# Idle products ahead of four norms and of the last down product, a tenth expert slot, and finer waits ahead of three expert loads

## What is computed

```python
for l in range(2):
    h = rmsnorm(x, g[0]);  y = mixer_l(h);           x = x + rmsnorm(y, g[1])
    h = rmsnorm(x, g[2]);  y = relu(h @ w1)**2 @ w2;  x = x + rmsnorm(y, g[3])
mod = silu(c) @ w_ada + b_ada                    # sh1, sc1, ga1, sh2, sc2, ga2
h  = modulate(rms_norm(x, g_norm1), sh1, sc1)
z  = h @ w_in;   merged = gate_a * (attn @ w_pa) + gate_b * (conv @ w_pb)
x  = x + ga1 * (merged @ w_o)
h2 = modulate(rms_norm(x, g_norm2), sh2, sc2)
x  = x + ga2 * moe(h2)      # 32 experts; silu(xb @ w1[e]) * (xb @ w3[e]) @ w2[e]
```

## Time and profile before

| | |
|---|---|
| median of 3 executions | 1529.51 us (1523.59, 1529.51, 1529.6) |
| the profiled execution, its own time | 1525.64 us |
| its span, first to last instruction | 1523.8 us |
| mean granted TensorE clock | 0.92 |
| TensorE busy, share of the span | 1283.0 us, 84% |
| VectorE busy | 557.2 us, 37% |
| ScalarE busy | 213.4 us, 14% |
| GpSimd busy | 83.5 us, 5% |
| DMA, mean over the span | 247 GB/s, 376.79 MB |
| expert loads (`<-in_w`) | 92 of 2048 KB and 8 of 1024 KB |

### The profile page before, as it was taken

One profiled execution on the slowest core, in us unless ns is written; L12 is line 12 of the kernel. 1 busy time (PEld: TensorE's weight loads), 2 busy tenths in 40 slices (PEclk: granted clock), 3 DMA queues, 4 the chain that ended last, 5 costly groups with the idle time before them and its releaser, 6 DMA issues.

```text
span 1523.8 us, 13457 instructions
## 1 busy us (share of the span) xinstructions
PE 1283.0 (84%) x5716; PEld 789.1 (52%) x5716; DVE 557.2 (37%) x732; ACT 213.4 (14%) x357; POOL 83.5 (5%) x77
## 2 busy tenths in 40 slices
PE   7999998999999988999999989998746646636646
PEld 4856747885446754888444778556312212212212
DVE  5478422546344732256436484415101001001001
ACT  3321211110011411111001123112100000000000
POOL 0047100000010001000001100000000000000000
PEclk9999998999999998999998999997878868778788
DMA  8633335884443333587543433476699999999996
GB/s 319 183 120 111 111 124 207 282 309 170 177 166 111 111 124 125 194 303 247 187 173 111 166 111 111 166 299 253 287 428 427 428 428 428 428 428 427 428 428 260
DMA packets 93611, 376.79 MB, mean 247 GB/s; under 512 B 6992, under 2 KB 7664, under 8 KB 81648
## 3 DMA queue, kind: packets, MB, share of 16 engines
q1 hardware_dynamic: 92832, 373.80, 63.5%
q0 software_dynamic: 576, 2.10, 0.4%
q10 hardware_dynamic: 144, 0.04, 0.0%
HBM read 374.88 MB, written 1.05 MB: 247 GB/s over the span
## 4 chain that ended last, share of the span: by engine, by line
PE 70%; DMA 19%; DVE 5%; SPq 2%; ACT 2%; issue 2%; POOL 1%; POOLq 0%; DVEq 0%; ACTq 0%
PE PS L853 15%; PE PS L863 13%; PE PS L665 11%; DMA weights<-in_w 10%; DMA proj_rows<-in_w 9%; PE PS L707 8%; PE PS L648 8%; PE PS L1074 5%; PE PS L1105 2%; PE PS L618 2%; SPq L483 1%; PE PS L1038 1%; PE PS L823 1%; PE PS L1046 1%; PE PS L764 1%
## 5 line engine op out<-in xcount | busy, mean ns | idle before, releaser
L853 PE MATMUL PS<-normalised,weights 128*128 128x256 f32 x1024 | 225.9, 384 | 1.6 <-DVE normalised L1495 1.6
L1074 PE MATMUL PS<-weights,arena 128*32 128x512 f32 x464 | 141.3, 710 | 90.0 <-DMA arena<-in_w 56.8
L853 PEld LDWEIGHTS PS<-normalised,weights 128*128 128x128 f32 x1024 | 197.5, 193 | 30.0 <-DVE normalised L1495 2.4
L863 PE MATMUL PS<-weights,arena 128*128 128x512 f32 x384 | 167.4, 592 | 0.0
L665 PE MATMUL PS<-weights,normalised 128*128 128x256 f32 x696 | 155.1, 380 | 3.2 <-DVE weights L1540 2.5
L665 PEld LDWEIGHTS PS<-weights,normalised 128*128 128x128 f32 x696 | 131.2, 190 | 24.9 <-issue 6.4
L648 PE MATMUL PS<-weights,normalised 128*128 128x512 f32 x288 | 131.0, 614 | 2.7 <-DVE normalised L1495 2.0
L707 PE MATMUL PS<-weights,arena 128*128 128x512 f32 x288 | 125.1, 594 | 4.9 <-issue 4.1
L1074 PE MATMUL PS<-arena 128*32 128x512 f32 x256 | 90.0, 733 | 45.7 <-DMA proj_rows<-in_w 22.8
L863 PEld LDWEIGHTS PS<-weights,arena 128*128 128x128 f32 x384 | 73.0, 190 | 91.0 <-issue 90.9
L2057 DVE TENSOR_TENSOR arena<-arena,PS 128x512 f32<-128x512 f32 x8 | 8.4, 1047 | 291.2 <-PE PS L1074 291.2
(11 more groups left out here) (314 smaller groups left out, 1447.3 us busy)
## 6 DMA issues: line engine op xcount, KB each, us to landing
weights<-in_w SPq DMA_DIRECT2D x40, 2048.0 KB, 26.1
weights<-in_mlp_w SPq DMA_DIRECT2D x32, 2048.0 KB, 7.8
arena<-in_w SPq DMA_DIRECT2D x22, 2048.0 KB, 25.0
proj_rows<-in_w SPq DMA_DIRECT2D x20, 2048.0 KB, 25.4
proj_rows<-in_w_ada SPq DMA_DIRECT2D x12, 2048.0 KB, 8.2
weights<-in_ev_w_in SPq DMA_DIRECT2D x10, 2048.0 KB, 8.4
weights<-in_w_in SPq DMA_DIRECT2D x10, 2048.0 KB, 7.9
normalised<-in_w SPq DMA_DIRECT2D x10, 2048.0 KB, 24.7
```

The lines of the kernel that those rows point to most:

```text
L853: last = mm(PS[:, 4 + 2 * h + j // 2, (j % 2) * T:(j % 2 + 1) * T], wn(s)[:, k, j * P:(j + 1) * P], HT[:, k, :], start=(k == 0), stop=(k = ...
L863: last = mm(PS[:, bank, :], lhs[:, k0 + i, rows], rhs[:, i, :], start=(g == 0 and i == 0), stop=(g == NGRP - 1 and i == 1))
L1074: last = mm(PS[CAP * x:CAP * (x + 1), 4 + kind, :], XG[:, k, CAP * x:CAP * (x + 1)], w[:, k, :], start=(k == 0), stop=(k == KT - 1), tile_ ...
```

## The change

- `keep_warm(bank, n)` issues n products of the identity with 512 columns of the constants into a bank of PSUM that nobody reads before it is written anew. It is called with n = 6 at the head of `mlp` (norms 1 and 3, bank 7), with 2 ahead of norm 2 and with 3 ahead of norm 4 (bank 6, after a wait on `y_rows`), and with 1 in the last group (bank 4).
- In the last group the scatter of the first half moves from behind the loop to a place ahead of the second half's down product, with the waits on `ex_swT` and `ex_y0`; behind the loop only the second half's is left.
- `MOE_SLOTS` has ten entries. The new slot 9 is 4096 columns of the array `arena` from column 2048 on. What lay there in the expert phase moves into the arrays of the residual rows, the head gains and the first gated rows.
- Expert blocks 4, 5 and 6 wait for the last `part_sum`, `merged` 2 and `mg_T` 3; blocks 7 and 8 for the two W_O blocks, block 9 for `h2_raw` 4. Before, 4 and 5 waited for `mg_T` 4, 6 and 7 for W_O, 8 for `h2_raw` 4.

```diff
--- before.py
+++ after.py
@@ -97,7 +97,7 @@
 QB = 3 * GRP
 MOE_BLOCKS = QUADS * QB
 
-MOE_SLOTS = (6, 7, 3, 1, 4, 5, 2, 0, 8)
+MOE_SLOTS = (6, 7, 3, 1, 9, 5, 4, 2, 0, 8)
 NSLOT = len(MOE_SLOTS)
 
 
@@ -298,17 +298,14 @@
         T4W = [quarter(PRF[:, K1:2 * K1]), quarter(PRF[:, 5 * K1:6 * K1])]
         YA1 = HT[:, 0:2, :].rearrange("p k t -> p (k t)")
         YSQ = [HT[:, 4:8, :].rearrange("p k t -> p (k t)"), PRF[:, K1:2 * K1]]
-        CWC = ar(5 * K1 + 256, TT, NE)
-        SEL = ar(5 * K1 + 320, TT, NE)
-        RK = ar(5 * K1 + 384, TT, NE)
+        CWC, SEL, RK = [HN[:, i * TT * NE:(i + 1) * TT * NE].rearrange("p (t e) -> p t e", t=TT) for i in range(3)]
         H2R = ar(0, TT, D)
-        XG = ar(2 * K1, KT, P)
-        SGU = ar(3 * K1, NB)
-        HIDR = ar(3 * K1 + 512, NB)
-        HIDT = ar(4 * K1, 4, P)
-        SWT = ar(4 * K1 + 512, T)
-        SEL1 = ar(4 * K1 + 768, TT, GRP, CAP)
-        SELW = ar(5 * K1, TT, GRP, CAP)
+        XG = X[:, 0, :].rearrange("p (k t) -> p k t", k=KT)
+        SGU, HIDR = X[:, 1, 0:NB], X[:, 1, NB:D]
+        HIDT = GA[:, 0, 0:NB].rearrange("p (k t) -> p k t", k=4)
+        SWT = GA[:, 0, NB:NB + T]
+        SEL1 = GA[:, 0, NB + T:D].rearrange("p (t e c) -> p t e c", t=TT, e=GRP)
+        SELW = HN[:, 512:768].rearrange("p (t e c) -> p t e c", t=TT, e=GRP)
         YSB = PRF[:, 2 * BW:2 * BW + D]
         RNDS = sb_i("rounds", P, 1)
         CS = ST[:, 104:112]
@@ -332,6 +329,8 @@
                 return PRF[:, (s - WSLOTS) * BW:(s - WSLOTS + 1) * BW]
             if s == WSLOTS + 4:
                 return XH[:, 0:BW]
+            if s == WSLOTS + 5:
+                return AR[:, 2 * K1:2 * K1 + BW]
             at = AR_END - (WSLOTS + 4 - s) * BW
             return AR[:, at:at + BW]
 
@@ -500,14 +499,17 @@
             sp.wait_ge(sem("block_used"), B_IN2_AT[9] + 1)
             expert_load(2)
             expert_load(3)
-            sp.wait_ge(sem("mg_T"), 4)
+            sp.wait_ge(sem("part_sum"), len(SEVEN))
             expert_load(4)
+            sp.wait_ge(sem("merged"), 2)
             expert_load(5)
+            sp.wait_ge(sem("mg_T"), 3)
+            expert_load(6)
             for c in range(2):
                 sp.wait_ge(sem("block_used"), B_WO + c + 1)
-                expert_load(6 + c)
+                expert_load(7 + c)
             sp.wait_ge(sem("h2_raw"), 4)
-            expert_load(8)
+            expert_load(9)
             round_loads(NSLOT, 0)
             n_rounds = rounds(sp)
             with sp.If(n_rounds > 1):
@@ -627,6 +629,11 @@
                     quad(4 + q, [XN[:, tt, (4 * half + j) * P:(4 * half + j + 1) * P] for j in range(4)])\
                         .then_inc(sem("xT_ready"), 1)
 
+            def keep_warm(bank, n):
+
+                for _ in range(n):
+                    mm(PS[:, bank, :], IDN, CK[:, 0:NB], start=True, stop=True)
+
             def open_rows(tt):
 
                 for half in range(2):
@@ -839,6 +846,7 @@
 
             def mlp(l, base, norm):
 
+                keep_warm(7, 6)
                 transpose_stream(norm)
                 pe.wait_ge(sem("hT_ready"), 4 * norm + 4)
 
@@ -888,6 +896,8 @@
             mlp(0, B_MLP0, 1)
 
 
+            pe.wait_ge(sem("y_rows"), 2)
+            keep_warm(6, 2)
             transpose_stream(2)
             proj_block(B_OD_IN, 2)
             seven_block(B_OD_IN + 1)
@@ -931,6 +941,8 @@
             mlp(1, B_MLP1, 3)
 
 
+            pe.wait_ge(sem("y_rows"), 4)
+            keep_warm(6, 3)
             transpose_stream(4)
             E0 = EV_IN + OD_IN
             proj_block(B_IN2_AT[0], 4)
@@ -1096,6 +1108,11 @@
                     arrived(2)
                 for half in range(2):
                     if last_quad:
+                        if half:
+                            pe.wait_ge(sem("ex_swT"), n + 1)
+                            pe.wait_ge(sem("ex_y0"), n + 1)
+                            scatter(0, True)
+                            keep_warm(4, 1)
                         pe.wait_ge(sem(f"last{half}_full"), r * (16 * GRP) + 16 * GRP)
                     else:
                         pe.wait_ge(sem(("ex_xg0", "ex_xg1")[half]), n + 2)
@@ -1114,10 +1131,8 @@
                 gather()
                 for q in range(QUADS):
                     quad_of_experts(q, r)
-                pe.wait_ge(sem("ex_swT"), r * QUADS + QUADS)
-                for half in range(2):
-                    pe.wait_ge(sem(("ex_y0", "ex_y1")[half]), r * QUADS + QUADS)
-                    scatter(half, True)
+                pe.wait_ge(sem("ex_y1"), r * QUADS + QUADS)
+                scatter(1, True)
 
 
         @block.scalar
```

## The result

Five executions took 1517.84, 1515.69, 1515.2, 1513.07 and 1514.97 us, median 1515.2; the kernel before, beside them, 1529.41. The ratio is 0.9922 with a 95% interval of 0.9909 to 0.9934: about 12 us faster, clear of the 0.5%. Forecast was 1518 us: 9.5 us less than the profiled execution of before, and half of the 3.9 us between that execution and the median added. The time is inside the range, the direction was right, and the gain was 2.4 us larger than the sum of 9.5.

A forecast was written before the change was run, and what follows sets the result against it. TensorE was taken to bound the first 29 slices and full DMA the expert phase. From 1525.64 us, -4.9 - 2.4 - 0.3 - 1.4 - 0.5 = -9.5 gave 1516.1; half of 3.9 added made 1518 us, range 1510 to 1526.

The forecast's parts named there:

- What bounds it: Whole kernel: TensorE sets the time in the first 29 slices, full DMA engines at 428 GB/s in the expert phase.
- The tenth slot: Expert phase: one 2.097 MB block moves from the full DMA stretch into an empty one, gain 4.9 us.
- Rival C: Expert stream: the slot gives nothing, the stream opening later or pausing; 1523 us, chance 0.08.
- The finer waits: Expert blocks 4 to 6: loads start up to some 18 us earlier, hidden by idle DMA, cost zero.
- The end: Last group: moved scatter and idle product keep TensorE busy, second half at full clock; gain 2.4 us, 0.7 if clock falls.
- Norms 2 and 4: Idle products ahead of these norms: gain 1.4 us at norm 2 and 0.5 at norm 4.
- I take 0.5: Norm 4, three idle products: gain 0.5 us, ends a loss of 2.7 and a gain of 2.15.
- Norms 1 and 3: Ahead of the MLPs: six idle products cost nothing, transposes do not hold the clock; gain 0.15 us each.
- The scale: Final time: half of the 3.9 us between profiled execution and median added to 1516.1, giving 1518 us.
- A: Norms 1, 3 and 4: transposes carry the clock, 5.75 us more gain than forecast; 1512 us, chance 0.2.
- B: Norms and last half: idle products give nothing, clock falls anyway, 5.6 us gain left; 1522 us, chance 0.22.
- D: Norms and end: idle products run at 1.2 GHz and outlast their gaps, slower; 1539 us, chance 0.04.

The follow-up runs named there:

- experiment 1: Kernel before plus only the idle products ahead of norms 1 to 4 (6, 2, 6 and 3): ratio 0.9961, median 1521.65 us.
- experiment 2: Kernel before plus only the tenth slot, the moved tiles and the finer waits: ratio 0.9972, 4.3 us faster.
- experiment 3: Kernel before plus only the first half's scatter moved ahead of the last wait and one idle product behind it: ratio 0.9983, 2.6 us faster.
- experiment 9: Whole change with the old single wait (mg_T 4) ahead of expert blocks 4, 5 and 6: ratio 0.9924 against the kernel before.
- Experiment 4: Whole change without the idle product ahead of the last wait, scatter still moved: ratio 0.9911 against the kernel before, median 1512.5 us.
- experiment 6: Kernel before plus only the idle products ahead of norms 2 and 4 (two and three): ratio 0.9991, 1.4 us faster.
- Experiment 5: Kernel before plus only the six idle products ahead of norms 1 and 3: ratio 0.9965, 5.3 us faster, median 1521.83 us.
- experiment 10: Whole change with three in place of six idle products ahead of norms 1 and 3: ratio 0.9948 against the kernel before.
- experiment 12: Whole change once more, unaltered, with a second profile: ratio 0.9924 against the kernel before, median 1515.2 us.
- experiment 7: Whole change plus four idle products (behind transposes of norms 1, 3, 4; around norm 5's), without the one ahead of the last wait: 0.9892, median 1511.86 us.
- experiment 11: Whole change plus four idle products (behind transposes of norms 1, 3, 4; around norm 5's), keeping the one ahead of the last wait: 0.9904, median 1512.42 us.
- Experiment 8: Whole change with twelve in place of six idle products ahead of norms 1 and 3: ratio 0.9962 against the kernel before.

## Why the prediction was right, and where it was not

**What bounds it: right.** TensorE sets the time up to the experts and DMA does in the expert phase, and the slot paid in the second, the norms in the first. The parts add up: experiments 1, 2 and 3 give 0.9961 x 0.9972 x 0.9983 = 0.9916, and the whole was measured at 0.9922 (0.9909 to 0.9934).

**The tenth slot, 4.9 us: right.** 4.8 in the profiles of after and of experiment 2, 4.3 (2.6 to 6.0) in the timed runs. Ten loads are out by 1058.82, and the first wait for a used block stands where it stood. Rival C falls.

**The finer waits, 0: right**, by experiment 9.

**The end, 2.4 us: right in size, wrong in one cause.** 2.5 in the profile, 2.6 in experiment 3. I had let the scatter and the idle product together keep TensorE busy up to the landing. Experiment 4 shows that the scatter does it alone; experiment 3 shows the product standing in front of the half, 0.5 us where the prediction said 0.3.

**Norms 2 and 4, 1.9 us: about right in the sum, wrong in the parts.** 1.4 in experiment 6, not clear of zero. Norm 4's "I take 0.5" was a quarter of what the profiles show, 2.15 us in all ten, the upper end that I had; norm 2's block gained 0.7 (14.65 to 13.97) and the modulation ahead of it lost up to 1.2 in some (its narrow products took 4.49 us in the chain of after and 4.61 in that of experiment 1, 3.46 in that of before). From MLP to MLP, norms 2 and 4 gain 0.5 and 2.2 us in the mean of five profiles with the change's products against three with none.

**Norms 1 and 3, 0.3 us: the step that failed.** "The rows speak against transposes as a cover": the row I read, 233.4 to 237.4 at 0.50, shows a clock that had already fallen and that transposes did not bring back. I used it as if it showed that transposes lose a clock that is still high. Those are two questions. With the pause of 5.68 us closed to 0.54 all sixteen transposes of norm 1 ran at full clock in six of six profiles, and the MLP's first products behind them in four. Experiment 5 puts both norms at 5.3 us (3.2 to 7.3), the difference of experiments 10 and 12 at 3.7. In the profiles norm 1's and norm 3's own stretches gain 2.9 us in the mean (1.2 and 1.0 in the MLPs' first products, which are held in some and not in others, and 0.4 and 0.3 because the MLP starts earlier behind the output product). So the profiles bear out ten times my 0.3, and the timed runs more than that; what is between 2.9 and 5.3 is not accounted for, beyond the width of the interval and what is told below of dips and of which executions were profiled. The page that I named (the Trainium skill, TensorE: Matmul & The Clock Gate, part 4, PE-mode transpose) says that transposes do not count as busy in the way products do. Experiment 10, where the clock falls in the middle of them, agrees with it, but does not show it; and while the clock was high the transposes ran at full clock (1.09 us for eight, 1.97 at the low one). The page has nothing on how short a stretch of them does no harm, and I let it decide.

**The scale.** I put half of the 3.9 us between the profiled execution and the median on top, without a reason for the half. Experiments 2 and 3, whose instructions are the same as before up to the third layer's end, show a part of those 3.9 us: both have a dip at 564 that makes the output product ahead of norm 3 29.9 and 30.1 us long, where the profile of before has 27.7. The profile of before was a good one of its kind.

**Rivals.** A (transposes carry the clock) was the nearest for the norms, though not every time; its 1512 us is what experiments 4, 7 and 11 reach. B falls with experiments 1 and 3 (6.0 and 2.6 us). D falls with the timelines: six products took 5.31 us in every profile, the two ahead of norm 2 took 1.9 to 2.5 us and the three ahead of norm 4 2.7 to 3.2, where D had 3.6 and 5.5. So some of these ran in part below full clock, but none outlasted its gap by more than tenths. Experiment 8 prices products beyond the gap at 6.1 us for twelve too many. Against D I had also written that PEclk is 1.00 in the idle stretch of norm 3; the rows do not show that one, and the trace of before has 0.93 there (595.7 to 601.6). It changed nothing.

## What to carry to other kernels

Where DMA is full, a further buffer is worth one block's transfer time and no more, and only if its load fits an idle stretch ahead of the full one; making the earlier waits finer gains nothing when those loads already land in idle time. Idle products pay where they close a pause in front of work at full clock. Here six products with 0.54 us left open ahead of norm 1's transposes held the clock in four profiles of six, three products with 3.11 us did not in the one profile; what lies between was not measured. One product more behind the transposes held it in both profiles that had it. Stay inside the gap, prefer real work moved forward (the scatter) to idle work, and judge by several executions, since one profile can miss the effect or double it. Do not read "this kind of work didn't bring the clock back" as "this kind of work lets it drop".

## What the runs showed of the hardware that was not expected

The profiles have dips of the granted clock to 0.50 at places where the instructions are unaltered, and not at the same places. The sixteen transposes ahead of norm 3's output product and that product, in before and then in after:

```profile
564.80 1.09 PE L618 MATMUL PS<-constants,proj_rows 128*128 128x128 f32 x8 [2.44 <-DVE proj_rows L1580]
566.07 1.09 PE L618 MATMUL PS<-constants,proj_rows 128*128 128x128 f32 x8 [0.17 <-DVE proj_rows L1580]
567.94 27.70 PE L707 MATMUL PS<-weights,arena 128*128 128x512 f32 x64 [0.78 <-issue]
```

```profile
562.11 3.23 PE L620 MATMUL PS<-constants,proj_rows 128*128 128x128 f32 x16 [2.45 <-DVE proj_rows L1595]
566.07 29.47 PE L714 MATMUL PS<-weights,arena 128*128 128x512 f32 x64 [0.73 <-issue]
```

The transposes and the start of the output product run at full clock in before; in after the clock falls among them (0.57 over the 6 us from 562, above). In the profiles one of two pieces is long, the block at 520 (15.7 to 16.8 in place of 14.0) or this output product (29.5 to 30.1 in place of 27.7), or both, and only in the profile of before neither. The time from the router's first product to the first group's is 24.4 to 24.6 us in some, 21.7 to 22.4 in others, and 23.1 or 23.2 in two. By the column of the first group's start, the five profiles with the change's products ahead of all four norms average 1066.8 us and the three with none 1072.3: 5.4 us. Cut into pieces, the four norms' own stretches make 5.6 of it, and the dips elsewhere nearly cancel in these five: 1.4 us lost at 520 and 1.4 between the third layer's start and its first output product, 1.9 gained between the router and the first group, and small pieces. In single profiles they don't cancel: that of after lost to them most of what its norms had gained, that of experiment 1 lost only a part. What decides where such a dip falls was not settled. The profiles of experiments 2 and 3 agree with each other within a few tenths up to 1070, and so do those of 9 and 12. But the change's own two profiles, of one and the same kernel, differ: norm 1 is 110.8 us in one and 112.5 in the other, the block at 520 14.0 and 15.7, the stretch from the router to the first group 24.4 and 22.1. So one kernel has its dips at different places in different executions. No run tells whether chance, the chip or a shift of the program decides it; nothing was run that shifts the program without adding products.

Which execution was profiled matters as well. Executions of one kernel can lie 4 us and more apart (1517.71 to 1527.05 in experiment 5, 1522.09 to 1526.62 in experiment 3). The profiled one was the fastest of its kernel in experiments 1, 4 and 8, and the slowest in after and in 7, 9, 10, 11 and 12. The two profiles with six products in which norm 3 was held are those of experiments 1 and 4. So "four of six" and "two of six" count these profiles; they are not the share of all executions.
